# A hybrid decoder layer on one core: more weight tiles asked for at once, channel sums on VectorE, and steps of the convolution branch and the experts moved

## Time and profile before

| | |
|---|---|
| three runs | 1317.44, 1317.88, 1321.84 us; median 1317.88 |
| profiled execution | 1319.82 us, span 1318.0 |
| busy | TensorE 1258.7 us (96%), VectorE 957.1 (73%), ScalarE 573.4 (44%), GpSimd 565.8 (43%) |
| mean granted TensorE clock | 0.974 of full |
| moved by the transfer engines | 273 MB, mean 207 GB/s |

### The profile page before, as it was taken

How to read it: one execution, slowest core, us unless ns; L and a number is a source line. 1 busy time by engine, 2 the same in 40 slices (tenths; PEclk the granted TensorE clock), 3 DMA queues, 4 the chain that set the end, 5 groups by cost and what they waited for, 6 DMA issues and landing times.

```text
span 1318.0 us, 27838 instructions
## 1 busy us (share of the span) xinstructions
PE 1258.7 (96%) x8645; PEld 1133.6 (86%) x8645; DVE 957.1 (73%) x2390; ACT 573.4 (44%) x988; POOL 565.8 (43%) x272
## 2 busy tenths in 40 slices
PE   5999999889998999989999999999999999999998
PEld 3767678777897989988999999999988888888887
DVE  2599933675434599999699999980166888888876
ACT  2200143444543444455455555554444555545552
POOL 0200024260264557788766666667600444435200
PEclk9999999889988999989999999999999999999999
DMA  9876454234443346645655555656777888888763
GB/s 356 273 242 210 154 193 172 96 117 131 142 129 135 129 129 201 208 154 178 200 184 183 180 183 183 182 181 212 249 257 251 295 321 320 295 316 293 286 236 132
DMA packets 114442, 273.14 MB, mean 207 GB/s; under 512 B 31376, under 2 KB 54640, under 8 KB 114000
## 3 DMA queue, kind: packets, MB, share of 16 engines
q1 hardware_dynamic: 99200, 243.76, 55.0%
q0 software_dynamic: 6432, 19.71, 4.2%
q10 hardware_dynamic: 8752, 8.93, 2.0%
HBM read 249.30 MB, written 23.00 MB: 207 GB/s over the span
## 4 chain that ended last, share of the span: by engine, by line
PE 86%; DVE 4%; issue 3%; POOL 2%; ACT 2%; DMA 1%; ACTq 1%; SPq 0%; POOLq 0%; DVEq 0%
PE ps L2072 18%; PE ps L1672 9%; PE ps L2075 9%; PE ps L2022 9%; PE ps L2015 9%; PE ps L2016 9%; PE ps L1709 5%; PE ps L1715 4%; PE ps L1721 4%; POOL split L661 2%; PE ps L2051 2%; PE ps L1737 1%; PE ps L1653 1%; PE ps L2000 1%; PE ps L1797 1%
## 5 line engine op out<-in xcount | busy, mean ns | idle before, releaser
L661 POOL TENSOR_TENSOR split<-ring,split 128x1024 fp32r<-128x1024 f32 x128 | 323.7, 2532 | 139.2 <-ACT split L959 139.2
L959 ACT ACTIVATE split<-ring 128x1024 fp32r<-128x1024 f32 x256 | 271.5, 1061 | 174.3 <-PE ps L2072 171.1
L2015 PE MATMUL ps<-h2r,split 128*128 128x288 f32 x1024 | 280.5, 298 | 5.3 <-ACT split L959 5.3
L2016 PE MATMUL ps<-h2r,split 128*128 128x288 f32 x1024 | 280.5, 298 | 0.0
L2072 PE MATMUL ps<-h2r,split 128*128 128x512 f32 x1024 | 257.4, 392 | 1.4 <-DVE h2r L1561 1.4
L2072 PEld LDWEIGHTS ps<-h2r,split 128*128 128x128 f32 x1024 | 184.2, 189 | 34.5 <-issue 1.6
L2015 PEld LDWEIGHTS ps<-h2r,split 128*128 128x128 f32 x1024 | 194.0, 189 | 6.0 <-ACT split L959 3.7
L626 POOL TENSOR_TENSOR split<-ring,split 128x1024 fp32r<-128x1024 f32 x48 | 118.6, 2473 | 181.5 <-ACT split L757 175.8
L2016 PEld LDWEIGHTS ps<-h2r,split 128*128 128x128 f32 x1024 | 193.6, 189 | 0.0
L2022 PE MATMUL ps<-h2r,split 128*128 128x288 f32 x1024 | 158.4, 297 | 5.5 <-POOL split L661 5.0
L1567 DVE TENSOR_TENSOR split<-ring,split 128x1024 fp32r<-128x1024 f32 x128 | 156.2, 1220 | 0.0
(11 more groups left out here) (264 smaller groups left out, 1631.0 us busy)
## 6 DMA issues: line engine op xcount, KB each, us to landing
ring<-in_stream SPq DMA_DIRECT2D x383, 512.0 KB
act_dram<-act SPq DMA_DIRECT2D x128, 128.0 KB, 1.8
parts<-act_dram SPq DMA_DIRECT2D x16, 512.0 KB
big<-act_dram SPq DMA_DIRECT2D x16, 512.0 KB
big<-in_stream SPq DMA_DIRECT2D x8, 512.0 KB, 10.2
big<-in_cache_k ACTq DMA_DIRECT2D x16, 128.0 KB, 3.4
big<-in_cache_v ACTq DMA_DIRECT2D x16, 128.0 KB, 3.2
s_act_dram<-act SPq DMA_DIRECT2D x128, 16.0 KB, 1.6
```

The source lines that it names most:

```text
L661: nc.gpsimd.tensor_tensor(split[:, n % 2, 1], ring[:, slot_of(n), :], split[:, n % 2, 0].bitcast(f32), ALU.subtract).then_inc(lo_ready, 1)
L959: nc.scalar.activation(split[:, n % 2, 0], ring[:, slot_of(n), :], ACT.Copy).then_inc(hi_ready, 1)
L2015: MM(out, u_hi[:, k], h_hi[:, k], start=(k == 0), stop=False)
L2016: last = MM(out, u_hi[:, k], h_lo[:, k], start=False, stop=False)
```

## The change

It has these parts:

1. `NWIDE` goes from 8 to 12, so 16 tiles are asked for without a wait; the place for them begins 2304 elements earlier, over `attn`.
2. ScalarE issues the four loads with `stateT` after its four copies of the modulation instead of before them.
3. VectorE sums the 8 chunks of x's squares, of y and of y's squares (`sum_chunks`, a reduction over a view whose inner step is 288 elements), and TensorE makes one matmul of each instead of eight. In stage `out` VectorE adds the squares of chunks 0 to 6 up, and TensorE makes two matmuls at the end.
4. y's reciprocal moves to n = 13 of the indexer's loop, and the multiplication, chunk by chunk, in front of the samples' indexer sums.
5. ScalarE's sigmoid of y comes after gate tile 2 instead of 1; TensorE's turning of the samples' scores after gate tile 0 instead of 1.
6. TensorE forms the samples' first rows at n = 0 instead of 1, in front of the first turning.
7. `SOFTMAX` goes from 20 to 28.

```diff
...
 BEFORE = 44
-SOFTMAX = 20
+SOFTMAX = 28
 TURN = BEFORE - R
-NWIDE = 8
+NWIDE = 12
 assert NWIDE % R == 0 and NWIDE + R <= NFIRST * R
...
         cache_i = early.take(NSEQ * NPAGES, PAGE)
-        wide_tiles = big[:, i_at - 2 * NSEQ * NPAGES * KV * PAGE:i_at][:, 0:NWIDE * D].rearrange("p (n c) -> p n c", c=D)
+        wide_at = i_at - 2 * NSEQ * NPAGES * KV * PAGE - KC * T
+        assert NWIDE * D <= early.at - wide_at
+        wide_tiles = big[:, wide_at:wide_at + NWIDE * D].rearrange("p (n c) -> p n c", c=D)
         wdw = early.take(KC, CW)
...
         causal = [causal_w[:, TP - P * (t + 1):] for t in range(NQ)]
+        over_x, over_y, over_yy = (gb[:, KV + 1 + n] for n in range(3))
         sq_qk = [gb[:, n] for n in range(KV)] + [attn[:, n] for n in range(H)]
...
+        chunk_sums = sem("chunk_sums")
...
+        y_normed = sem("y_normed")
...
             root(1)
-            for dst, src in ((staged_s, "stateT"), (wdw, "wdw"), (cvec, "cvec"), (qkg, "qkg")):
-                eng.dma_start(dst, a[src]).then_inc(conv_in, 16)
                 nc.scalar.activation(m_row[:, i], lin[i % 2][:, 0:P], ACT.Copy).then_inc(ada_copied, 1)
+            for dst, src in ((staged_s, "stateT"), (wdw, "wdw"), (cvec, "cvec"), (qkg, "qkg")):
+                eng.dma_start(dst, a[src]).then_inc(conv_in, 16)
...
                 evac(("gate_b", n), gb[:, n], ACT.Sigmoid)
-                if n == 1:
+                if n == 2:
...
                 eng.wait_ge(x1_ready, 3 * k + 3)
-                nc.scalar.activation(xn[:, k], x[:, k], ACT.Square).then_inc(squares2, 1)
+                nc.scalar.activation(pa[0][:, 0:T] if k == 0 else xn[:, k], x[:, k], ACT.Square).then_inc(squares2, 1)
             eng.wait_ge(x1_ready, 3 * KC)
...
             V.tensor_tensor(cs[:, :, 0:NG], cs[:, :, 0:NG], cT, ALU.mult).then_inc(c_silu, 1)
+            def sum_chunks(dst, src):
+                V.tensor_reduce(dst, src[:, :, :].rearrange("p k t -> p t k"), AX.X, ALU.add).then_inc(chunk_sums, 1)
+            dve.wait_ge(squares, 1)
+            sum_chunks(over_x, xn)
             root(1)
...
                 .then_inc(y_sample, 1)
+            dve.wait_ge(y_prompt, KC)
+            dve.wait_ge(y_sample, 1)
+            sum_chunks(over_y, y)
...
                     V.scalar_tensor_tensor(v, v, gain, pa[2 + m % 2][:, 0:T], ALU.mult, ALU.mult).then_inc(qk_ready, 1)
+                if n == 11:
+                    dve.wait_ge(squares, 2)
+                    sum_chunks(over_yy, xn)
+                if n == 13:
+                    root(2)
                 if n == 7:
...
                                             ALU.mult, ALU.add))
+            dve.wait_ge(y_centred, 1)
+            settle()
+            for k in range(KC):
+                V.tensor_tensor(y[:, k], y[:, k], rstd, ALU.mult).then_inc(y_normed, 1)
...
-            dve.wait_ge(y_centred, 1)
-            root(2)
-            step(V.tensor_tensor(y[:, :, :], y[:, :, :], over_chunks(rstd), ALU.mult))
-            settle()
+            dve.wait_ge(y_normed, KC)
             for k in range(KC):
...
                 residual(n, (bank[:, 0:TP], bank[:, TP:T]), mod[:, 2], x, x, bank[:, TP:T], x1_ready)
+                if n >= 2:
+                    dve.wait_ge(squares2, n)
+                    settle()
+                    if n < KC - 1:
+                        step(V.tensor_tensor(pa[0][:, 0:T], xn[:, n - 1], pa[0][:, 0:T], ALU.add))
+                    else:
+                        V.tensor_tensor(xn[:, 0], xn[:, n - 1], pa[0][:, 0:T], ALU.add).then_inc(chunk_sums, 1)
...
-            def sums(src, out, n):
-                for k in range(n):
-                    last = MM(out[:, 0:T], ones[:, :], src[:, k], start=(k == 0), stop=(k == n - 1))
-                return last
+            def sums(src, *last_src):
+                every = (src, *last_src)
+                for n, part in enumerate(every):
+                    last = MM(stb[:, 0:T], ones[:, :], part, start=(n == 0), stop=(n == len(every) - 1))
+                last.then_inc(stats, 1)
...
-                    pe.wait_ge(squares, 1)
-                    sums(xn, stb, KC).then_inc(stats, 1)
+                    pe.wait_ge(chunk_sums, 1)
+                    sums(over_x)
                 if i % 2 == 1:
...
-                    pe.wait_ge(y_prompt, KC)
-                    pe.wait_ge(y_sample, 1)
+                    pe.wait_ge(chunk_sums, 2)
                     pe.wait_ge(qk_root, 1)
-                    sums(y, stb, KC).then_inc(stats, 1)
+                    sums(over_y)
                 if n == 12:
-                    pe.wait_ge(squares, 2)
-                    sums(xn, stb, KC).then_inc(stats, 1)
+                    pe.wait_ge(chunk_sums, 3)
+                    sums(over_yy)
                 if n % 2 == 0:
...
                 linear_cut(("gate_b", n))
-                if n == 1:
+                if n == 0:
                     pe.wait_ge(s_summed, 2)
...
-                if n in (1, 3):
+                if n in (0, 3):
...
-            for n in range(KC + 1):
-                if n < KC:
-                    linear_cut(("out", n))
-                if n:
-                    pe.wait_ge(squares2, n)
-                    last = MM(stb[:, 0:T], ones[:, :], xn[:, n - 1], start=(n == 1), stop=(n == KC))
-            last.then_inc(stats, 1)
+            for n in range(KC):
+                linear_cut(("out", n))
+            pe.wait_ge(chunk_sums, 4)
+            pe.wait_ge(squares2, KC)
+            sums(xn[:, 0], xn[:, KC - 1])
```

## The result

The changed kernel took **1297.37 us**, the median of 4 runs (1294.92 to 1302.61), beside 1318.64 (1317.44 to 1321.84) for the kernel before; the ratio is 0.984, with a 95% interval of 0.9805 to 0.9876. The forecast was 1294.9 us, with a range of 1288 to 1307. The changed kernel scatters more than the one before: two repeats further down had medians of 1303.31 and 1301.87, and all 13 runs together have 1301.29, with every one of them between 1294.92 and 1304.89. Against the kernel before beside each group the gain is 21.3, 15.7 and 16.5 us, so it is some 16 to 21, and the forecast gain of 23 was too good by 2 to 7.

The account below looks back on a forecast made before the run. TensorE, holding 86% of the span, was taken as the bound; gains of 4.3, 3.6, 1.9, 5.0, 2.6, 2.4 and 3.2 sum to 23.0 us, from median 1317.88 to 1294.9, range 1288 to 1307.

Parts of the forecast that it names:

- rival (a): Start, samples' rows and exponentials give nothing, as earlier starts are caught up further on; 12.9 us remain: 1305.0; chance 0.17.
- VectorE's chain, 5.0: Chain to the softmax: reciprocal and multiplications of y move into idle time, less a sigmoid wait of 2.6; 5.0 us gained.
- Rival (d): Deferring the sigmoid makes a VectorE wait of 2.6 us instead of saving one; already in the sum, no separate chance.
- rival (b): The sigmoid of y comes so late that VectorE's chain gains nothing: 18.0 us gained, 1299.9; chance 0.08.
- Samples' rows, 2.6: Before the first turning: samples' rows cover TensorE's wait for the first normed row; 2.6 us gained, bounds 0 and 3.
- Sums of y, 3.6: TensorE's line: eight matmuls summing y become one, VectorE's added reduction lies in idle time; 3.6 us gained.
- Squares of y, 1.9: Indexer stretch: 3.6 us leave TensorE, but it waits 1.7 for VectorE's 4.3 us reduction; 1.9 us gained.
- rival (c): Reductions at the 1152-byte stride cost far more than at 128, making the kernel slower, 1327.6 at 22 us each; chance 0.03.
- Start, 4.3: Kernel start: sixteen tiles asked for at once, state behind them, end TensorE's waits for weights earlier; 4.3 us gained.
- Stage `out`, 2.4: Stage `out`: seven small matmuls leave TensorE's line, VectorE adds squares while waiting; 2.4 us gained, bounds 1 and 2.9.
- Exponentials, 3.2: Expert scores: exponentials eight tiles later end the waiting for the top-k; 3.2 us gained, bounds 1 and 4.9.
- an unbroken wait for `picks` of several us: Profile sign listed as wrong; the forecast expected `picks` no more than 2 us ahead of TensorE.

Follow-up runs that it names:

- the run with early exponentials and late turning: Changed kernel with exponentials back behind expert tile 19 (SOFTMAX 20) and the turning of `picks` four tiles later (BEFORE 48): 1301.21 us, ratio 0.9871.
- the late turning: Changed kernel with the turning of `picks` and the gate work behind it four expert tiles later (BEFORE 48 instead of 44): 1297.53 us, ratio 0.985.
- the first repeat: The changed kernel measured again without edit, beside the kernel before: 1303.31 us, ratio 0.9875; its profiled execution took 1296.67.

## Why the prediction was right, and where it was not

The sign and the range held, and the time missed by 2.5 us against the first four runs and by 6.4 against all 13. The 2.5 are partly luck: the first four runs have the lowest of the changed kernel's three medians. By the time alone rival (a), 1305.0, is nearer to the median of all 13 (3.7 us) than the forecast; the rows decide between them. What the start and the samples' rows gained was not caught up further on (undone, they cost 3.1 and 2.9 us in the profiles), so (a) held for the exponentials only. Against its own execution the sum of 23.0 stands beside 17.2 measured. Step by step:

- **VectorE's chain, 5.0.** Right in size (5.0), and rightly the largest term: undone, it costs 8.4 us, as the samples' rows then wait as well. Two of its items were off by 2 us each against each other: GpSimd's cut hit the scaling (+2.1), so the sigmoid was waited for 0.6 us and not 2.6. Rival (d), a wait made by the deferral, is hardly there; rival (b) fell, the sigmoid did not come too late.
- **Samples' rows, 2.6.** Right: 2.7 in the table, 2.9 undone. The terms are not additive: VectorE's chain and these rows undone one at a time cost 11.3 together, while the whole change gained 7.7 there. Part of that is the eight multiplications under two cuts, which the kernel before did not have; that the rest is each step covering what the other exposes is my reading.
- **Sums of y, 3.6.** The run with the squares on TensorE leaves 46.52 - 43.05 = 3.5 from the first q/k spread (196.21 before, 193.17 in that run) to the `wi` spread. Right; no run took this step back by itself.
- **Squares of y, 1.9.** The reduction (4.35 us for 4.3 forecast) and its wait (1.38 for 1.7) were right, so rival (c), the dear stride, is out. With the half clock taken off the term is 2.0, right; in the profiles only 0.4 is left of it. The term counted the wait's own length and no change of the clock. The clock's mean in 220 to 242 us is 0.77 in eight of the eleven executions with the wait and 0.85 in the run without it, but 0.92 in the run with early exponentials and late turning, which has the same wait. Whether the wait is the cause stays open.
- **Start, 4.3.** 2.8 in the first profile and 3.6 in both repeats, whose clock was full there. The step "12.98 + 12 x 1.26" took the transfer time of the last tiles for all twelve; the first seven took 1.54 each. That the state's lateness costs nothing held, though it landed only at 44 us, far later than I had thought.
- **Stage `out`, 2.4.** 2.3 by the experiment; the rest of the 4.4 in the table is the clock in the kernel before.
- **Exponentials, 3.2.** The failed step: "at most 4.9 can be had, less when the first product no longer finds GpSimd idle (+2.1 on VectorE)" looked at the first product alone (which did find GpSimd idle, 2.29 us) and took it that `picks` moves with everything ahead of it. TensorE's side was right: it arrives at 612.52, 23.6 us earlier than before, 4.5 more than at the first expert tile. But `picks` moved only 14.0, as the end of the top-k met a GpSimd that had been idle there before: 7.6 us. So the term became a loss of 1.9, outside its bounds of 1 and 4.9. In the repeat that was hit less it is a gain of 1.6 against the kernel before, and with the late turning the 3.2 are there. Rival (a) had named the place, `picks` ending the wait last, but not that the chain to it would grow. Of the recorded signs of being wrong, "an unbroken wait for `picks` of several us" came, 4.90.

What stays open: why the slow clock comes at different places in executions of one kernel. The repeats differ from the first profile in the start by 1.7 us for that reason alone.

## What to carry to other kernels

When a change takes a wait from one engine, ask which third engine had stood still during that wait, and whose short operations had run undisturbed because of it: here ScalarE's wait kept GpSimd quiet, and VectorE's chain of small casts paid for its end. Take the chain of dependence that was nearly late ("4.9 us to spare") and price every row of it again under the new neighbours, not only its first. And move the consumer away, by a few tiles, in the same change.

## What the runs showed of the hardware that I had not expected

- Not only VectorE's long products of two operands are held by GpSimd's cuts. A cast of 0.27 us took 2.50, a shift of integers 2.41, a copy of three 128x8 pieces 1.29 instead of 0.31, eight multiplications of 128x288 with a scalar pair 4.87 instead of 2.81. Each of these rows is the longer by up to the length of one cut (2.4 us); six casts in the first repeat met two and took 5.19 us instead of 0.89. The Trainium skill (SBUF — State Buffer, section Who interferes with whom) lists copy, cast and `tensor_scalar` among the operations that can take the ports shared with GpSimd, under a lock held for the whole instruction; these rows agree. The prediction had used the same rule for the two-operand products alone. The max, find and replace operations in the same stretch (264 to 406 ns each, the same in both kernels) did not pay.
- A reduction over chunks 1152 bytes apart took 4.08, 4.16 and 4.35 us for 2304 elements, 1.77 to 1.89 ns each, a little less than the 2.06 at 128 bytes: the larger stride is not dearer.
- The granted clock fell to 0.5, the lower of its two levels (1.2 GHz), at places that differ between executions of one kernel: in one it is 1.00 up to 232 us and 0.50 from there to 242, in another 0.6 in 222 to 226, 1.00 to 232, about 0.55 to 240 and 1.00 again. With GpSimd's cuts falling on more or fewer of VectorE's short operations, that makes the 5.9 us between the first profile and the first repeat: 2.5 up to the first `gate_a` tile by the clock, 3.5 in the expert stage. All 13 runs of this one program lie between 1295 and 1305 us.
